# A bidirectional delta rule on one Trainium2 core: its triangular inverses in 32x32 blocks instead of 64x64

## What is computed

```python
gc = jnp.cumsum(gch, -1)
decay = jnp.exp(jnp.where(tril, gc[..., :, None] - gc[..., None, :], -jnp.inf))
m = jnp.where(strict, jnp.einsum('bhncd,bhnsd->bhncs', kb, kc) * decay, 0.0)
tmat = lax.linalg.triangular_solve(m + eye, jnp.broadcast_to(eye, m.shape), left_side=True,
                                   lower=True, unit_diagonal=True)
u = jnp.einsum('bhncs,bhnsv->bhncv', tmat, vb)
w = jnp.einsum('bhncs,bhnsk->bhnck', tmat, kb * jnp.exp(gc)[..., None])
qk = jnp.einsum('bhncd,bhnsd->bhncs', qc, kc) * decay
def step(s, inp):
    v_new = u_i - jnp.einsum('bhck,bhkv->bhcv', w_i, s)
    o_i = jnp.einsum('bhck,bhkv->bhcv', qd_i, s) + jnp.einsum('bhcs,bhsv->bhcv', qk_i, v_new)
    s = s * gl_i[..., None, None] + jnp.einsum('bhck,bhcv->bhkv', kd_i, v_new)
    return s, o_i
```

## Time and profile before

| what | us |
|---|---|
| median of 3 runs (lowest to highest) | 3326.49 (3324.87 to 3326.53) |
| the profiled execution's own time | 3332.55 |
| its span, from first to last instruction | 3330.8 |
| the stage of the delta rule, first level to last o | 1383.3 to 1755.5 |

### The profile page before, as it was taken

How to read it: one execution, slowest core, us unless ns; L and a number is a source line. 1 busy time by engine, 2 the same in 40 slices (tenths; PEclk the granted TensorE clock), 3 DMA queues, 4 the chain that set the end, 5 groups by cost and what they waited for, 6 DMA issues and landing times.

```text
span 3330.8 us, 54983 instructions
## 1 busy us (share of the span) xinstructions
PE 3126.7 (94%) x23540; PEld 2541.3 (76%) x23540; DVE 1662.1 (50%) x2684; ACT 1191.9 (36%) x2158; POOL 307.6 (9%) x312
## 2 busy tenths in 40 slices
PE   7989998989998999899988899999999988999998
PEld 5767887757776787789885578888888766678886
DVE  3255445354535545767756555333344456653444
ACT  4315335365531553422224344111112435641221
POOL 1020020000002100243431000000000101000000
PEclk8999999989999999999999999999999999999999
DMA  5283212270327231222211003112121323032231
GB/s 213 76 323 111 101 59 101 101 253 26 99 86 280 76 108 51 73 103 72 97 44 42 26 14 89 64 51 76 52 76 51 100 58 70 8 95 83 94 114 64
DMA packets 175005, 306.56 MB, mean 92 GB/s; under 512 B 19270, under 2 KB 40583, under 8 KB 174505
## 3 DMA queue, kind: packets, MB, share of 16 engines
q1 hardware_dynamic: 147008, 278.71, 24.9%
q0 software_dynamic: 3712, 12.74, 1.3%
q10 hardware_dynamic: 24041, 11.60, 1.3%
HBM read 294.87 MB, written 6.80 MB: 91 GB/s over the span
## 4 chain that ended last, share of the span: by engine, by line
PE 73%; DVE 15%; ACT 8%; issue 2%; DMA 1%; POOL 0%; ACTq 0%; DVEq 0%; SPq 0%
PE psum L425 18%; PE psum L427 17%; PE psum L426 17%; PE psum L2373 5%; PE psum L958 3%; PE psum L583 2%; DVE small L1122 2%; PE psum L977 2%; ACT feat L692 2%; DVE weights_r L369 2%; DVE arena L875 1%; DVE x_lat L878 1%; PE psum L992 1%; PE psum L2365 1%; PE psum L2437 1%
## 5 line engine op out<-in xcount | busy, mean ns | idle before, releaser
L369 DVE TENSOR_TENSOR weights_r<-weights,weights_r 128x2048 fp32r<-128x2048 f32 (+1 forms) x166 | 361.0, 2195 | 500.9 <-ACT weights_r L360 500.8
L425 PE MATMUL psum<-feat_r,weights_r 128*128 128x512 f32 (+1 forms) x1536 | 538.4, 351 | 9.6 <-DVE feat_r L722 4.9
L425 PE MATMUL psum<-weights_r,feat_r 128*128 128x512 f32 (+2 forms) x1344 | 526.1, 391 | 12.7 <-DVE weights_r L369 8.4
L426 PE MATMUL psum<-feat_r,weights_r 128*128 128x512 f32 (+1 forms) x1536 | 536.3, 349 | 0.0
L427 PE MATMUL psum<-feat_r,weights_r 128*128 128x512 f32 (+1 forms) x1536 | 535.5, 349 | 0.0
L360 ACT ACTIVATE weights_r<-weights 128x2048 fp32r<-128x2048 f32 (+1 forms) x166 | 302.7, 1845 | 630.0 <-DMA weights<-in_w_ffn_gate 204.3
L427 PE MATMUL psum<-weights_r,feat_r 128*128 128x512 f32 (+2 forms) x1344 | 520.2, 387 | 0.0
L426 PE MATMUL psum<-weights_r,feat_r 128*128 128x512 f32 (+2 forms) x1344 | 519.9, 387 | 0.0
L425 PEld LDWEIGHTS psum<-feat_r,weights_r 128*128 128x128 f32 x1536 | 293.4, 191 | 54.0 <-issue 5.5
L427 PEld LDWEIGHTS psum<-feat_r,weights_r 128*128 128x128 f32 x1536 | 293.0, 191 | 36.9
L426 PEld LDWEIGHTS psum<-feat_r,weights_r 128*128 128x128 f32 x1536 | 293.2, 191 | 36.3
(11 more groups left out here) (476 smaller groups left out, 4416.5 us busy)
## 6 DMA issues: line engine op xcount, KB each, us to landing
weights<-in_w_mod SPq DMA_DIRECT2D x48, 2048.0 KB, 13.0
weights<-in_gla_w_in SPq DMA_DIRECT2D x24, 1024.0 KB, 7.3
weights<-in_w_ffn_gate SPq DMA_DIRECT2D x20, 1024.0 KB, 7.3
weights<-in_w_ffn_up SPq DMA_DIRECT2D x20, 1024.0 KB, 5.0
weights<-in_w_ffn_down SPq DMA_DIRECT2D x20, 1024.0 KB, 6.2
weights<-in_fox_w_in SPq DMA_DIRECT2D x16, 1024.0 KB, 7.1
weights<-in_sgu_w_in SPq DMA_DIRECT2D x12, 1024.0 KB, 6.4
weights<-in_gla_w_out SPq DMA_DIRECT2D x8, 1024.0 KB, 6.7
```

The lines of the kernel that those rows point to most:

```text
L369: dve.e.tensor_tensor(WEI_r[:, s * SLOT:s * SLOT + n], WEI_t[:, s * SLOT:s * SLOT + n], WEI_r[:, s * SLOT + HALF:s * SLOT + HALF + n].bitc ...
L425: pe.e.matmul(ps, lh, rh, start=first, stop=False)
L426: pe.e.matmul(ps, lh, rl, start=False, stop=False)
```

## The change

The diagonal blocks of the inverse become 32x32, four on the partitions (STRIPS), with four levels after the first in place of five. A level is 32 matmuls for v and 32 for X^T, of 32x32 each; X itself is no longer made by matmuls: DVE subtracts into X^T and turns the result over in 32x32 blocks (STREAM_TRANSPOSE). `pe_xt`, the matmuls with the identity, is gone. The blocks are joined to 64x64 by `pe_join_v` (16 matmuls) and `pe_join_z` (24), which ACT evicts, then cross and corner as before, with the eviction of the corner moved from DVE to ACT. All joins, cross and corner of step n - 1 now stand in step n, and every v is parted from its z by another product. Other edits: beta is multiplied in along with k times k, in eight instructions a step of 128 columns; the triangle mask is added while clamping (values of -1e30) and the second clamp is a Relu on ACT, so two DVE passes over 1024 columns each go away; DU has three buffers, its reload stands in the middle of a step, and the difference and clamp are made two steps ahead; POOL's masks are half as wide and its copies are ten of 32 partitions by 256 columns where there were four of 64 by 512.

```diff
-    DD, DU = own[0:3], [own[3], own[6]]
-    Cc = [own[7][:, 0:512], own[7][:, 512:1024]]
-    XC, XTC = ([x[:, c:c + 512] for x in (own[4], own[8])] for c in (0, 512))
-    VC, MC = own[5][:, 0:512], own[5][:, 512:1024]
+    DD, DU = own[0:3], [own[3], own[6], own[8]]
+    XX = [own[4][:, n * 512:(n + 1) * 512].rearrange("p (w h c) -> p w h c", w=2, h=8) for n in range(2)]
+    VX, XN = own[5][:, 0:512], own[5][:, 512:1024]
+    Cc = [own[7][:, n * 256:(n + 1) * 256] for n in range(2)]
+    VC, MC = own[7][:, 512:768], own[7][:, 768:1024]
...
-    def pe_blocks(pe, out_, lhsT, rhs, heads, name, halves=(lo_, hi_)):
-        for h in heads:
-            for rows in halves:
-                done = pe.e.matmul(out_[rows, (h - heads[0]) * 64:(h - heads[0] + 1) * 64], lhsT[rows, h, :],
-                                   rhs[rows] if len(rhs.shape) == 2 else rhs[rows, h, :], start=True, stop=True)
+    def pe_strips(pe, out_, lhsT, rhs, name):
+        for h in range(4):
+            for rows in STRIPS:
+                done = pe.e.matmul(out_[rows, h * 32:(h + 1) * 32], lhsT[rows, h, :], rhs[rows, h, :], start=True, stop=True)
         done.then_inc(*B.put(name))
-    def pe_xt(pe, n):
-        ps = K.open(pe, (D_, "xt", n))
-        pe.wait_ge(*V.of((D_, "x", n)))
-        pe_blocks(pe, ps, h8(XC[n % 2]), IDENT_C, range(8), (D_, "xt", n))
-    def pe_level(pe, n, level):
-        C, X, Xt = Cc[level % 2], XC[n % 2], XTC[n % 2]
+    def pe_v(pe, n, level):
+        C = b2(h8(Cc[level % 2]))
         for hb in range(2):
             at = (D_, "v", n, level, hb)
             ps = K.open(pe, at)
             pe.wait_ge(*G.of((D_, "C", n, level)))
-            pe.wait_ge(*(A if level == 1 else V).of((D_, "x level", n, level - 1, hb)))
-            pe_blocks(pe, ps, h8(C), h8(Xt), range(4 * hb, 4 * hb + 4), at)
+            pe.wait_ge(*V.of((D_, "x level", n, level - 1, hb)))
+            pe_strips(pe, ps, C[:, hb], XX[n % 2][:, 0, 4 * hb:4 * hb + 4, :], at)
+    def pe_z(pe, n, level):
         for hb in range(2):
+            at, v, x = (D_, "z", n, level, hb), b2(h8(VC))[:, hb], XX[n % 2][:, 1, 4 * hb:4 * hb + 4, :]
+            ps = K.open(pe, at)
             pe.wait_ge(*A.of((D_, "v", n, level, hb)))
-            for l_, r_, which in ((X, VC, "xt"), (VC, X, "x")):
-                at = (D_, "z", n, level, hb, which)
-                ps = K.open(pe, at)
-                pe_blocks(pe, ps, h8(l_), h8(r_), range(4 * hb, 4 * hb + 4), at, x_halves(n, level, which))
+            pe.wait_ge(*V.of((D_, "x turned", n, level - 1, hb)))
+            pe_strips(pe, ps, x, v, at)
+    def pe_join_v(pe, n):
+        at = (D_, "join v", n)
+        ps = K.open(pe, at)
+        for hb in range(2):
+            pe.wait_ge(*V.of((D_, "x level", n, 4, hb)))
+        for h in range(8):
+            for a in range(2):
+                near, far = strips_of(n, a)
+                done = pe.e.matmul(ps[near, h * 32:(h + 1) * 32], h8(DU[n % 3])[far, h, near],
+                                   XX[n % 2][far, 0, h, :], start=True, stop=True)
+        done.then_inc(*B.put(at))
+    def pe_join_z(pe, n):
+        at = (D_, "join z", n)
+        ps, v = K.open(pe, at), h8(VX[:, 0:256])
+        pe.wait_ge(*A.of((D_, "join v", n)))
+        for hb in range(2):
+            pe.wait_ge(*V.of((D_, "x turned", n, 4, hb)))
+        for h in range(8):
+            x = XX[n % 2][:, 1, h, :]
+            for a in range(2):
+                near, far = strips_of(n, a)
+                done = pe.e.matmul(ps[near, h * 32:(h + 1) * 32], x[near], v[near, h, :], start=True, stop=True)
+                if a == near_half(n):
+                    done = pe.e.matmul(ps[far, h * 32:(h + 1) * 32], v[near, h, :], x[near], start=True, stop=True)
+        done.then_inc(*B.put(at))
...
+    def act_decay_relu(act, n):
         act.wait_ge(*V.of((D_, "clamped", n)))
-        act.e.activation(DU[n % 2], DU[n % 2], ACT.Exp, scale=-1.0).then_inc(*A.put())
-        act.e.activation(DD[n % 3], DD[n % 3], ACT.Exp).then_inc(*A.put((D_, "decays", n)))
+        act.e.activation(DU[n % 3], DU[n % 3], ACT.Relu).then_inc(*A.put())
+    def act_decay_exp(act, n):
+        act.chain()
+        act.e.activation(DU[n % 3], DU[n % 3], ACT.Exp, scale=-1.0).then_inc(*A.put((D_, "decays u", n)))
...
-        dve.e.tensor_scalar(DD[n % 3], dif, 0.0, None, ALU.min).then_inc(*V.put())
-        dve.chain()
-        dve.e.tensor_scalar(dif, dif, 0.0, None, ALU.max).then_inc(*V.put((D_, "clamped", n)))
-    def dve_kq(dve, n, which):
+        dve.e.scalar_tensor_tensor(h8(DD[n % 3]), h8(DU[n % 3]), 0.0, rows_over(NEG[order[n][0]], 8), ALU.min,
+                                   ALU.add).then_inc(*V.put((D_, "clamped", n)))
+    def dve_kk(dve, n):
         d, t = order[n]
-        mine = h8((DU[n % 2], DD[n % 3])[which])
+        M = h8(DU[n % 3])
+        dve.wait_ge(*A.of((D_, "decays u", n)))
+        dve.wait_ge(*B.of((D_, "kq", n, 0, 1)))
         for par in range(2):
-            at = (D_, "kq", n, which, par)
-            dve.wait_ge(*B.of((D_, "kq", n, which, 1)))
-            dve.wait_ge(*A.of((D_, "decays", n)))
+            at = (D_, "kq", n, 0, par)
+            for h in range(par, 8, 2):
+                dve.e.scalar_tensor_tensor(M[:, h, :], K.at[at][:, h // 2 * P:(h // 2 + 1) * P],
+                                           BETA[:, t, d * 8 + h:d * 8 + h + 1], M[:, h, :], ALU.mult,
+                                           ALU.mult).then_inc(*V.put(K.frees(V, at), (D_, "m", n)))
...
     def dve_level(dve, n, level):
         for hb in range(2):
-            half = slice(hb * 256, (hb + 1) * 256)
-            dve.wait_ge(*B.of((D_, "z", n, level, hb, "x")))
+            at = (D_, "z", n, level, hb)
+            Xt, X = (flat(XX[n % 2][:, w, 4 * hb:4 * hb + 4, :]) for w in range(2))
+            dve.wait_ge(*B.of(at))
             dve.chain()
-            for dst, which in ((XTC[n % 2], "xt"), (XC[n % 2], "x")):
-                at = (D_, "z", n, level, hb, which)
-                some = x_halves(n, level, which)
-                rows = slice(some[0].start, some[-1].stop)
-                dve.e.tensor_tensor(dst[rows, half], dst[rows, half], K.at[at][rows, 0:256],
-                                    ALU.subtract).then_inc(*V.put(K.frees(V, at)))
-            V.mark((D_, "x level", n, level, hb))
-    def dve_corner(dve, n):
-        near, far = near_far(n)
-        at = (D_, "corner", n)
-        dve.wait_ge(*B.of(at))
-        dve.e.tensor_scalar(h8(XT[order[n][0]])[near, :, far], h8(K.at[at])[near], -1.0, None,
-                            ALU.mult).then_inc(*V.put(K.frees(V, at), at))
+            dve.e.tensor_tensor(Xt, Xt, K.at[at][:, 0:128], ALU.subtract).then_inc(
+                *V.put(K.frees(V, at), (D_, "x level", n, level, hb)))
+            dve.chain()
+            dve.e.transpose(X, Xt).then_inc(*V.put((D_, "x turned", n, level, hb)))
...
+    def pool_assemble(pool, n):
+        X, a = h8(XT[order[n][0]]), near_half(n)
+        for hb in range(2):
+            pool.wait_ge(*V.of((D_, "x turned", n, 4, hb)))
+        if n >= 2:
+            pool.wait_ge(*B.of((D_, "u", n - 2)))
+        pool.chain()
+        for rows in STRIPS[2 * (1 - a):2 * (1 - a) + 2]:
+            pool.e.tensor_copy(X[rows, :, rows], XX[n % 2][rows, 0]).then_inc(*G.put((D_, "XT far", n)))
+        for s, rows in enumerate(STRIPS[2 * a:2 * a + 2]):
+            pool.e.tensor_copy(h8(XN)[rows, :, 32 * s:32 * s + 32], XX[n % 2][rows, 1]).then_inc(*G.put((D_, "XN", n)))
+        pool.chain()
+        for rows in STRIPS[2 * a:2 * a + 2]:
+            pool.e.tensor_copy(X[rows, :, rows], XX[n % 2][rows, 0]).then_inc(*G.put((D_, "XT", n)))
...
```

More of the change, by code:

```diff
@@ L2336, in near_far, with strips_of, near_half @@
         return (lo_, hi_) if order[n][0] == 0 else (hi_, lo_)
-    def x_halves(n, level, which):
-        return near_far(n)[0:1] if which == "x" and level == LEVELS - 2 else (lo_, hi_)
+    def strips_of(n, a):
+        two = STRIPS[2 * a:2 * a + 2]
+        return two if order[n][0] == 0 else two[::-1]
+    def near_half(n):
+        return order[n][0]
     def pe_gdn_begin(pe):
@@ L2399, in pe_cross @@
         ps = K.open(pe, (D_, "cross", n))
-        for hb in range(2):
-            pe.wait_ge(*V.of((D_, "x level", n, LEVELS - 2, hb)))
+        pe.wait_ge(*A.of((D_, "join z", n, "far")))
+        pe.wait_ge(*G.of((D_, "XT far", n)))
         for h in range(8):
-            done = pe.e.matmul(ps[near, h * 64:(h + 1) * 64], h8(DU[n % 2])[far, h, near], h8(XTC[n % 2])[far, h, :],
+            done = pe.e.matmul(ps[near, h * 64:(h + 1) * 64], h8(DU[n % 3])[far, h, near], h8(XT[order[n][0]])[far, h, far],
                                start=True, stop=True)
@@ L2507, in act_level, with act_join_v, act_join_z, act_cross @@
             act.chain()
-            act.e.activation(VC[:, hb * 256:(hb + 1) * 256], K.at[at][:, 0:256],
+            act.e.activation(VC[:, hb * 128:(hb + 1) * 128], K.at[at][:, 0:128],
```

(67 more changed lines are left out.)

231 lines of the change are left out of this document (121 added, 110 removed).

## The result

| | before | changed |
|---|---|---|
| median us (lowest to highest, runs) | 3327.68 (3321.07 to 3337.25, 20) | 3310.29 (3291.99 to 3327.91, 20) |
| ratio, 95% interval | | 0.9942 (0.9927 to 0.9958) |
| the profiled execution's own time | 3332.55 | 3311.9 |
| first level to last o | 1383.3 to 1755.5 | 1381.9 to about 1732 |

What follows compares the result with a forecast made beforehand. PE, busy 94% of the span, was taken as the bound: 117 us less PE work, 15 us of waits and 1 us of ends gave -101 us, 3231.5 profiled, 3226 as median; 8-in-10 range 3195 to 3305.

Steps and rivals of the forecast that it cites:

- The rate of the small matmuls: PE's four levels per step: 512 instructions of 32x32 at 10 ns each, 5.1 us; bounds 7.3 and 29 ns.
- Rivals 1 and 2: PE's small matmuls: starts stay at 29 ns, 3356 us, chance 0.12; or 15 to 20 ns, 3256 to 3291, chance 0.14.
- Waits on other engines: PE's round trips between v, z and the next v: 1.25 us charged per step, 15 us in all.
- DVE was right: DVE's work per step: 16.6 us against 21.5 before, staying under PE's 20.3 with its waits.
- Rival 3: DVE becomes the bound if turnings cost 0.62 us and multiplications 0.48: +56 us, 3282; chance 0.12.
- Rival 4: PE's clock falls to 1.2 GHz in light bursts with waits: +229 us, 3455, if for the whole stage; chance 0.05.
- the ends: After the last level: two bare joins and evictions add about 4 us, a 2.72 us wait goes; net +1 us.

Runs made afterwards that it cites:

- e7: The kernel before the change, plus one PE halt per step ahead of level 4 (eight useless 32x32 matmuls, each waited for): 3383.94 us, ratio 1.0161.
- e9: e8 plus one useless 384-column matmul ahead of each of join z, cross, corner, u and o in the last step: 3282.34 us, ratio 0.9854.
- e5: The changed kernel with the four heads' small matmuls streaming 128, 96, 64 and 32 columns instead of 32 each: 3289.41 us, ratio 0.9883.
- e6: The changed kernel with the four heads' small matmuls streaming 64, 64, 64 and 32 columns instead of 32 each: 3300.23 us, ratio 0.9903.
- e8: e5 with DVE's read of the side's fold moved ahead of vb, the difference and the clamp: 3290.48 us, ratio 0.9878.

## Why the prediction was wrong

**The rate of the small matmuls was right.** 10 ns were taken, between 7.3 and 29. 64 in 0.75 us, with some 0.19 us until the last result stands, are 8.8 ns, and the forecast asked for 0.7 to 0.8. That holds over whole bursts between the supply halts wherever the clock was full. It lies near the 7.3 ns worked out from a tile's own rate; the prediction's other ground, that PE starts a load and a matmul in 7 ns, was more than its rows show, which have loads 7 ns apart but matmuls up to 15. Rivals 1 and 2 fall, and with them the rule of about 25 ns from start to start of the Trainium skill's "TensorE: Matmul & The Clock Gate", "Wait — 56ns, not 53.3ns?", for matmuls on four different tiles.

**Waits on other engines were oversized, and another kind was missing.** 15 us were charged for round trips. PE waited about 1 us for DVE, ACT and POOL from 1395 to 1700 us, but 19 us for issue. The sum is about right, which is luck, as the cause is wrong: the halts stand behind the transfers of instructions, about 255 to a transfer, where the bursts take a matmul with its load in 9 ns. The prediction's "the products of whole tiles in between leave time to queue the next" is the sentence that failed.

**DVE was right.** The groups of the changed kernel, 1380 to 1745 us:

```profile
L2730 DVE STREAM_TRANSPOSE feat<-feat 128x128 f32<-128x128 f32 x96 | 29.9, 311 | 3.3
L2727 DVE TENSOR_TENSOR feat<-feat,psum 128x128 f32<-128x128 f32 x96 | 27.6, 288 | 120.0 <-PE psum L2388 114.7 <-DVE feat L2730 0.5
L2562 ACT ACTIVATE weights<-psum 128x128 f32<-128x128 f32 x96 | 26.6, 277 | 104.4 <-PE psum L2388 98.8
...
L2693 DVE SCALAR_TENSOR_TENSOR weights<-psum,small,weights 128x128 f32<-128x128 f32 x64 | 17.3, 344 | 7.2 <-PE psum L2378 7.1
```

A turning takes 311 ns where 290 were taken (bounds 220 to 620), the multiplications 344 for 300, ACT's copy 277 for 280. DVE's 120 us of idle time ahead of L2727 are ended by PE, as foreseen, and DVE is busy for 195 us of the stretch, 249 before. Rival 3 falls.

**The clock is the step that failed.** Rival 4 had named it and was given 0.05, with the argument "waits here would be under 1 us each". That was read from semaphores alone, and the halts at which the clock fell are of 1.3 to 2.8 us. It was also taken that the work between halts would bring the clock back, as in the kernel before, where the bursts had twice the columns. e7 gives 0.37 us for each low us. The single runs of the changed kernel give nearly the same: of 20, the one at a mean clock of 0.950 over the span took 3292.0, the one at 0.937 took 3327.9, and a line through all 20 has 0.34 us for each us of low time (correlation 0.93). The 206 more low us then make 70 to 76 us, and 3226 gets to 3296 to 3302 of the 3310 measured. So the clock, a term that the sum put at nothing, is 70 to 76 of the 84 us that were missing; the other 8 to 14 are not told apart, and the ends below are part of them. Rival 4's own price was too high: it doubled all of PE's work, but a burst goes only from 0.75 to 1.07 us. So it put the point of no gain at 44% of the stage, and with 224 low us in a stage of 350 (64%) the kernel is still 0.6% faster.

**The ends were undersized.** +1 us was forecast. The bare joins and what follows ran wholly at 1.2 GHz in the changed kernel, and PE waits 0.5 to 0.9 us ahead of each of five pieces, 3.5 us together:

```profile
1721.61 1.97 PE L2451 MATMUL psum<-feat 64*64 64x64 f32 x16 [0.68 <-ACT feat L2594]
1724.31 3.65 PE L2475 MATMUL psum<-rows,weights 128*128 128x64 f32 x16 [0.73 <-issue]
1728.64 3.67 PE L2483 MATMUL psum<-arena,feat 128*128 128x64 f32 x16 [0.69 <-ACT arena L2607]
```

The corner alone takes 1.97 us for 1.09. In e9 the last u takes 1.97 and the last o 2.00 us, with a filler ahead of each. Most of this loss is the clock's and is counted above.

**What stays open.** Whether 32-column bursts would let the clock fall without any halt: at 1433.2 us of the changed kernel it fell with no halt of more than 0.4 us in the 12 us ahead of it, and that one case is not explained. Whether it is the columns of each instruction that count, or that a burst takes longer with them, no run parts: e5 and e6 change both. Whether fewer instructions, and so fewer fetches, would end the halts was not tried.

## What to carry to other kernels

Work taken out of a burst is won only while the clock stays up: price a change that makes matmuls smaller and more numerous at both clocks, and look at the granted clock, since PE's busy share of the span stays at 94% either way. A halt of 2.4 us in dense work (e7) cost three quarters as much again through the clock, and in the light bursts of this kernel a low piece was four times as long on average (21 us for 5). Where small matmuls are needed, more columns per instruction can be cheaper than fewer, even if the surplus is thrown away, as e5 and e8 show.

## What was not expected of the hardware

- Four 32x32 tiles take f32 matmul instructions 8.8 ns apart over whole bursts at 2.4 GHz, and about 13 ns at 1.2 GHz ((1.07 - 0.24) / 64, where 0.24 us is the time until the last result stands there).
- PE halts for up to 2.5 us in a run of short instructions and goes on 1.2 to 1.5 us after the end of a transfer of 0.02 MB on the instruction queue, which takes 0.9 to 1.4 us; in 305 us the changed kernel has 63 of these, the one before 52.
- 2.4 us of single small matmuls in otherwise dense work lower the clock for 3.4 or 6.8 us right behind them (12 of 12 in e7).
- Adding 55 us of matmul columns made the program 21 us faster.
